# Experts' weights asked for by two engines: wide pairs by SyncE, narrow pairs by ScalarE, and the last unit's narrow pairs in places of wide ones

## The chip, the core and the metric

The kernel runs on one core of one Trainium2 chip. The metric is the device time of one launch in microseconds, the median over runs. Engines are named as in the profile: PE is TensorE (PEld its weight loads), DVE is VectorE, ACT is ScalarE, POOL is GpSimd, SP is SyncE.

## The reference

Three transformer-like blocks follow each other on 256 tokens of width 1024, in float32. The change lies in the second block's mixture of experts: a router picks 4 of 32 experts for each token, and each expert is two dense layers with a clipped SwiGLU between them.

```python
N_EXPERTS = 32
TOP_K = 4
D_FF_EXPERT = D_MODEL          # 1024
SWIGLU_ALPHA = 1.702
SWIGLU_LIMIT = 7.0
```

The first layer of an expert (`exp_w1`) is 1024 x 2048 (8 MB), the second (`exp_w2`) is 1024 x 1024 (4 MB). Each is multiplied once with the rows that the router sent to that expert, which are few, so that the 12 MB of weights of an expert are the larger cost to bring in.

## The kernel before

**Units.** The experts are worked through in units of up to 64 tokens. There are 32 units here, one for each expert (an expert with more than 64 tokens would add a unit). Unit `u` has a wide half (`widen`, the first layer, matmuls on line 2958) and a narrow half (`narrow`). The narrow half adds the previous unit's result into the output (`scatter`, line 2933), gathers the tokens of a later unit (line 2904), turns the hidden values (line 2986), and then multiplies with the second layer (line 3004). Between the wide half and the matmuls of line 3004, DVE and ACT clip, gate and copy; the last step of this is ACT's copy on line 3176.

**Weights in pairs.** The weights of a unit are twelve panels, moved as six pairs of 2 MB each, 128 partitions x 16 KB. Pairs 0 to 3 are wide, pairs 4 and 5 narrow (`TWICE` = 4, `PAIRS` = 6). The ring has ten places: pairs 0 to 3 have a place for even units and another for odd units, and pairs 4 and 5 have one place each for all units. Pairs 0 to 2 of even units lie in `ring`, which other stages use as six slots of 1 MB; all others lie in `expert_ring`. A transfer may start when PE has used up what was in the place before: PE raises `used` after each panel, 12 to a unit. PE waits for a pair on the semaphore of its place.

**Who asks.** Every weight transfer is asked for by SP, in the order in which its program has them, each behind its own wait for `used`. Up to unit 18 a turn of SP's loop has the wide pairs of one parity first, then the narrow pairs; from `AHEAD` = 9 pairs of units on (`in_turn`) a turn has the narrow pairs of the next unit first:

```python
def in_turn(v, before, even, odd):
    load(sp, v * 2 - 2, once, 1, before)
    load(sp, v * 2 - 2, twice, 0, even)
    load(sp, v * 2 - 1, once, 0, even)
    load(sp, v * 2 - 1, twice, 1, odd)
```

`load(sp, turn, pairs, odd, e)` waits until unit `turn` has used each of the `pairs` and then asks for the same pair of expert `e` into its place. `once` are pairs 4 and 5, `twice` are pairs 0 to 3. So the narrow pairs of unit u + 1 are asked for when unit u has used its own, and the wide pairs of unit u + 2 when unit u has used its own and SP has come past the narrow ones ahead of them. The transfers asked for by SP are one queue (q1 of the profile), those asked for by ACT are another (q10).

**The end.** The last unit (31) has odd places. Its narrow pairs are the last two weight transfers. Behind them SP asks for the first six panels (1 MB each, `w_in`) of the third block, into all six slots of `ring`. The third block starts when the last `scatter` is added.

Of the kernel before, what the change touches and what calls it, by code (L numbers as in the profile page):

```python
# [22 lines left out]
RING = 6  # L23
# [2817 lines left out]
def mixture_of_experts(core, h, halves_of_y, modulation, bias, ring, rw):  # L2841
# [3 lines left out]
    E, S = N_EXPERTS, UNIT  # L2845
# [5 lines left out]
    with ExitStack() as s:  # L2851
# [18 lines left out]
         glu_ready, sig_ready, hid_ready, hid_turned, hid_copied, bias_used, copied, scattered, added, turn) = (  # L2870
            core.counter("expert_" + n) for n in names)

        def pair_count(eng):
            return eng.value_load(unit_int[0:1, MAX_UNITS:MAX_UNITS + 1], min_val=E // 2, max_val=MAX_UNITS // 2)

        def last_pair(eng):
            return eng.value_load(unit_int[0:1, MAX_UNITS + 1:MAX_UNITS + 2], min_val=E // 2 - 1, max_val=MAX_UNITS // 2 - 1)

# [80 lines left out]
                                       start=False, stop=(j == 7))  # L2959
                mm.then_inc(used.sem, 1)  # L2960

        def panel(pe, u, v, odd, j):
            if j % 2 == 0:
                sig = ring.loaded_at(j // 2, odd)
                pe.wait_ge(sig.sem, (v if j // 2 < TWICE else u) * 16 + 16)
            return ring.panel(j, odd)

        def narrow(pe, u, v, odd, first=False, final=False):

            if not first:  # L2970
                scatter(pe, u)

            if not final:
                pe.wait_ge(picked.sem, picked.at(u + 2))
                gather(pe)
            pe.wait_ge(gates_picked.sem, gates_picked.at(u + 1))
            for b in range(NB):
                mm = pe.transpose(ps[:, 7, b * P:b * P + P], selg[:, b, :], ident)
            mm.then_inc(gates_turned.sem, 1)
            if first:  # L2980
                turn_columns(pe)
            pe.wait_ge(hid_ready.sem, hid_ready.at(u + 1))
            if not final:
                pe.wait_ge(xt_ready.sem, xt_ready.at(u + 2))
            for c in range(4):
                mm = pe.transpose(ps[:, 6, c * P:c * P + P], lin[:, c * P:c * P + P], ident)
            mm.then_inc(hid_turned.sem, 1)

            if not first:
                pe.wait_ge(added.sem, added.at(u * 4 + 1))  # L2990
            for out, at in halves:
                mm = pe.matmul(ps[out, 2, :], pick[:, :], bias[:, 2 * D + at:2 * D + at + 512], start=True, stop=False)
            mm.then_inc(bias_used.sem, 1)
            pe.wait_ge(gates_copied.sem, gates_copied.at(u + 1))
            if not final:
                turn_gathered(pe, u + 2)
            pe.wait_ge(hid_copied.sem, hid_copied.at(u + 1))
            for q in range(4):
                w = panel(pe, u, v, odd, 8 + q)
                for i in range(2):  # L3000
                    k = 2 * q + i
                    at_k = k % 4 * P + k // 4 * S
                    for out, at in halves:
                        mm = pe.matmul(ps[out, 2, :], hidt[:, at_k:at_k + S], w[:, i * D + at:i * D + at + 512],  # L3004
                                       start=False, stop=(k == DT - 1))
                mm.then_inc(used.sem, 1)

        def load(sp, turn, pairs, odd, e):
            for q in pairs:

                sp.wait_ge(used.sem, turn * PANELS + (2 * q + 2))
                sp.dma_start(ring.pair(q, odd), ring.weights(e, q)).then_inc(ring.loaded_at(q, odd).sem, 16)
        twice, once = range(TWICE), range(TWICE, PAIRS)

        def sb2(name, shape, dt=F32):
# [43 lines left out]
        with core.block() as block:  # L3059
# [85 lines left out]
            @block.scalar  # L3145
            def _(act):
                act.dma_start(rw[:, :, :], core.a["router"]).then_inc(core.const_loaded.sem, 16)
                core.load_table(act, ACT.Sqrt)
                act.wait_ge(gains_ready.sem, gains_ready.at(1))
                for k in range(DT):  # L3150
                    act.wait_ge(kept.sem, kept.at(k + 1))
                    act.activation(gained_tile[k], x[:, k, :], ACT.Copy, scale=core.gain[:, k:k + 1]).then_inc(gained.sem, 1)
                    if k < DT - 1:
                        act.activation(squares[:, k, :], x[:, k, :], ACT.Square).then_inc(squared.sem, 1)
                act.wait_ge(var_ready.sem, var_ready.at(1))
                act.activation(rs[:, :], rs[:, :], ACT.Sqrt).then_inc(rooted.sem, 1)
                act.wait_ge(rooted.sem, rooted.at(2))
                for half in range(2):
                    act.wait_ge(turned.sem, turned.at(half + 1))
                    for b in range(NB):  # L3160
                        act.activation(ht[:, b, 512 * half:512 * half + 512], ps[:, 2 * half + b, :], ACT.Copy,
                                       scale=rs[:, b:b + 1]).then_inc(copied_ht.sem, 1)
                copy_gathered(act, 1)
                act.wait_ge(shifted.sem, shifted.at(1))
                for b in range(NB):
                    ins = act.activation(g[:, b, :], lg[:, b, 0:E], ACT.Exp, bias=sm[:, b, 0:1])
                ins.then_inc(exped.sem, 1)
                core.load_table(act, ACT.Sigmoid)
                act.wait_ge(counted.sem, counted.at(1))
                def unit(u, final=False):  # L3170
                    act.wait_ge(glu_ready.sem, glu_ready.at(u + 1))
                    act.activation(sg[:, :], glu[:, :], ACT.Sigmoid, scale=SWIGLU_ALPHA).then_inc(sig_ready.sem, 1)  # L3172
                    if not final:
                        copy_gathered(act, u + 2)
                    act.wait_ge(hid_turned.sem, hid_turned.at(u + 1))
                    act.activation(hidt[:, :], ps[:, 6, :], ACT.Copy).then_inc(hid_copied.sem, 1)
                last = last_pair(act)
                with act.Fori(0, last) as v:
                    for odd in range(2):
                        unit(v * 2 + odd)  # L3180
                unit(last * 2)
                unit(last * 2 + 1, final=True)
                core.load_table(act, ACT.Sqrt)

# [141 lines left out]

            @block.sync
            def _(sp):
                def expert(u):
                    return sp.value_load(unit_int[0:1, bass.ds(u, 1)], min_val=0, max_val=E - 1)  # L3330
                issue_panels(core, sp, len(core.stream))
                ring.load_rest(sp)
                core.used += 4
# [1 line left out]
                    sp.wait_ge(used.sem, n + 1)  # L3335
                    sp.dma_start(ring.pair(0)[:, n * SLOT:n * SLOT + SLOT], ring.weights(2, 0)[:, n * SLOT:n * SLOT + SLOT]).then_inc(sig.sem, 16)
                load(sp, 0, twice[1:], 0, 2)
                load(sp, 0, range(4, PAIRS), 1, 1)
                load(sp, 1, twice, 1, 3)
                load(sp, 1, once, 0, 2)  # L3340
                with sp.Fori(2, AHEAD) as v:
                    load(sp, v * 2 - 2, twice, 0, v * 2)
                    load(sp, v * 2 - 2, once, 1, v * 2 - 1)
                    load(sp, v * 2 - 1, twice, 1, v * 2 + 1)
                    load(sp, v * 2 - 1, once, 0, v * 2)

                def in_turn(v, before, even, odd):
                    load(sp, v * 2 - 2, once, 1, before)
                    load(sp, v * 2 - 2, twice, 0, even)
                    load(sp, v * 2 - 1, once, 0, even)  # L3350
                    load(sp, v * 2 - 1, twice, 1, odd)
                load(sp, AHEAD * 2 - 2, twice[:1], 0, AHEAD * 2)
                load(sp, AHEAD * 2 - 2, once, 1, AHEAD * 2 - 1)
                load(sp, AHEAD * 2 - 2, twice[1:], 0, AHEAD * 2)
                load(sp, AHEAD * 2 - 1, once, 0, AHEAD * 2)
                load(sp, AHEAD * 2 - 1, twice, 1, AHEAD * 2 + 1)
                with sp.Fori(AHEAD + 1, E // 2 - 1) as v:
                    in_turn(v, v * 2 - 1, v * 2, v * 2 + 1)
                sp.wait_ge(counted.sem, counted.at(2))
                n = pair_count(sp)  # L3360
                with sp.Fori(E // 2 - 1, n) as v:
                    in_turn(v, expert(v * 2 - 1), expert(v * 2), expert(v * 2 + 1))
                last = last_pair(sp)
                load(sp, last * 2, once, 1, expert(last * 2 + 1))

                sp.wait_ge(used.sem, last * (2 * PANELS) + RING)
                switch_stream(core, STREAM_2)
                issue_panels(core, sp, RING)
        core.const_loaded.close(16)


PANELS, PAIRS, TWICE, AHEAD = 12, 6, 4, 9


class ExpertRing:
# [22 lines left out]
    def panel(self, j, odd=0):  # L3398
        return self.pair(j // 2, odd)[:, j % 2 * SLOT:j % 2 * SLOT + SLOT]
# [640 lines left out]
```

## Time and profile before

| what | value |
|---|---|
| median of 3 runs | 2319.06 us (2317.56 to 2319.47) |
| the profiled execution's own time | 2318.64 us |
| its span | 2316.8 us |
| granted TensorE clock, mean over the span | 0.995 |
| PE busy, whole span | 2217.1 us (96%) |
| DVE, ACT, POOL busy | 923.0, 382.1, 435.6 us |
| weight transfers of the experts | 144 + 47 pairs of 2 MB, and two of 1 MB |

The profiled execution's own time is 1.8 us above its span and 0.4 us below the median. The experts' units run from 1139.7 to 2050.6 us of the span. PE's busy share is an average over stages: what a change in the experts is worth is read in that stretch alone, from what PE waits for there and from how full the DMA engines are. Matmuls are counted as instructions; one float32 matmul of the program leaves two of them.

### The profile page before, as it was taken

To read this page: it belongs to the slowest core of one execution; us is meant where nothing else is said; L and a number is where in the kernel's file an instruction comes from. 1 tells how busy PE (TensorE), PEld (TensorE's weight loads), DVE (VectorE), ACT (ScalarE), POOL (GpSimd) and SP (SyncE) were. 2 spreads that over 40 slices of the span, in tenths; PEclk is the share of its full clock that TensorE was granted. 3 is DMA by queue.
4 is the path that set the end of the run, shared out by engine and by line. 5 is a ranking of instruction groups with operands and counts; after the bars stand their busy time and mean duration, and the time that the engine had idled before them with its cause. 6 is when DMAs were issued, how large, how long until landed. Compare 5 with 4: busy or idle time off the path is not lost. (4 is left out here: it accounts for less than half of the span.)

```text
span 2316.8 us, 35106 instructions
## 1 busy us (share of the span) xinstructions
PE 2217.1 (96%) x14557; PEld 1516.7 (65%) x14557; DVE 923.0 (40%) x1961; ACT 382.1 (16%) x856; POOL 435.6 (19%) x365
## 2 busy tenths in 40 slices
PE   8999999999999998999999999999999999999997
PEld 7888899987799987887633333333333333368786
DVE  4242465645444564626333333322333333252322
ACT  2210130124211023225200000000000000023321
POOL 0120498820088850012000000000000000000000
PEclk9999999999999999999999999999999999999999
DMA  7334754464864554323699999999999999953322
GB/s 264 128 125 145 239 168 164 161 234 170 326 217 164 164 182 163 120 111 152 247 426 427 428 428 428 428 428 427 405 426 430 426 429 428 427 238 130 127 82 82
DMA packets 61155, 619.36 MB, mean 267 GB/s; under 512 B 6800, under 2 KB 8080, under 8 KB 12304
## 3 DMA queue, kind: packets, MB, share of 16 engines
q1 hardware_dynamic: 59328, 611.08, 66.3%
q10 hardware_dynamic: 1712, 6.63, 0.8%
q8 instruction: 87, 1.43, 0.2%
q14 instruction: 28, 0.23, 0.0%
HBM read 616.63 MB, written 1.05 MB: 267 GB/s over the span
## 5 line engine op out<-in xcount | busy, mean ns | idle before, releaser
L2958 PE MATMUL ps<-expert_ring,moe_xg 128*64 128x512 f32 x1280 | 281.8, 593 | 9.8 <-DMA expert_ring<-we_dram 9.6
L3004 PE MATMUL ps<-expert_ring,mix_y 128*64 128x512 f32 x1024 | 228.5, 596 | 11.2 <-DMA expert_ring<-we_dram 11.2
L2958 PEld LDWEIGHTS ps<-expert_ring,moe_xg 128*64 128x64 f32 x1280 | 90.5, 137 | 189.8 <-issue 167.5
L466 PE MATMUL ps<-x_res,ring 128*128 128x256 f32 x896 | 201.3, 383 | 8.6 <-DMA x_res<-x_dram 8.6
L466 PEld LDWEIGHTS ps<-x_res,ring 128*128 128x128 f32 x896 | 169.8, 192 | 33.0 <-DMA ring<-w_in_dram 8.5
L3270 DVE TENSOR_SCALAR mix_y<-ps 128x512 f32<-128x512 f32 x32 | 22.1, 692 | 421.5 <-PE ps L2958 421.5
L2775 POOL COPY unscaled_x<-modulations 128x8 f32<-128x8 f32 x1 | 0.2, 198 | 936.0 <-POOLq L3059 936.0
L2958 PE MATMUL ps<-ring,moe_xg 128*64 128x512 f32 x768 | 168.2, 593 | 0.5 <-DVE moe_xg L2919 0.3
L3004 PEld LDWEIGHTS ps<-expert_ring,mix_y 128*64 128x64 f32 x1024 | 69.9, 137 | 147.4 <-issue 127.0
L466 PE MATMUL ps<-third_h,ring 128*128 128x256 f32 x704 | 160.1, 383 | 1.3 <-DVE third_h L3855 1.0
L625 POOL TENSOR_TENSOR seven_weights<-ring 128x512 f32<-128x512 f32 (+1 forms) x72 | 94.1, 1307 | 325.8 <-DVE seven_x_turned L641 289.1
L466 PEld LDWEIGHTS ps<-third_h,ring 128*128 128x128 f32 x704 | 133.8, 192 | 21.6 <-issue 2.2
L3172 ACT ACTIVATE mix_y<-mix_y 128x512 f32<-128x512 f32 x32 | 20.1, 630 | 739.8 <-DVE mix_y L3270 739.8
L2958 PEld LDWEIGHTS ps<-ring,moe_xg 128*64 128x64 f32 x768 | 54.6, 137 | 105.2 <-issue 98.9
L626 POOL TENSOR_TENSOR ring<-ring 128x512 f32<-128x512 f32 (+1 forms) x72 | 105.1, 1460 | 0.0
L430 PE MATMUL ps<-x_res,ring 128*128 128x128 f32 x768 | 102.1, 276 | 0.2
L430 PE MATMUL ps<-seven_x_turned,seven_weights 128*128 128x128 f32 x768 | 102.0, 276 | 0.2
L430 PE MATMUL ps<-seven_x_turned,ring 128*128 128x128 f32 x768 | 101.7, 275 | 0.2
L2943 DVE SCALAR_TENSOR_TENSOR x_res<-ps,modulations,x_res 128x256 f32<-128x256 f32 x248 | 99.7, 476 | 0.0
L466 PE MATMUL ps<-expert_ring,ring 128*128 128x256 f32 x416 | 95.3, 386 | 4.3 <-ACT expert_ring L279 4.3
L628 POOL TENSOR_TENSOR seven_weights<-seven_weights,ring 128x512 f32<-128x512 f32 (+1 forms) x72 | 98.2, 1363 | 0.0
L430 PEld LDWEIGHTS ps<-x_res,ring 128*128 128x128 f32 x768 | 93.7, 192 | 1.9 <-issue 0.8
(625 smaller groups left out, 3315.2 us busy)
## 6 DMA issues: line engine op xcount, KB each, us to landing
expert_ring<-we_dram SPq DMA_DIRECT2D x144, 2048.0 KB, 22.5
ring<-we_dram SPq DMA_DIRECT2D x47, 2048.0 KB, 25.6
ring<-w_in_dram SPq DMA_DIRECT2D x55, 1024.0 KB, 4.8
ring<-ffn_up_dram SPq DMA_DIRECT2D x44, 1024.0 KB, 5.1
ring<-ada_dram SPq DMA_DIRECT2D x36, 1024.0 KB, 4.8
ring<-w_out_dram SPq DMA_DIRECT2D x16, 1024.0 KB, 5.0
ring<-ffn_dn_dram SPq DMA_DIRECT2D x16, 1024.0 KB, 5.0
ring<-ple_g_dram SPq DMA_DIRECT2D x8, 1024.0 KB, 6.5
```

The costliest lines, as they stand in the source:

```text
L430: mm = pe.matmul(core.ps[:, bank, at:at + P], seven.weight(w, f, half, product, p), seven.moving(panel, sources[panel], k0, half, product, ...
L466: mm = pe.matmul(core.ps[:, bank_of[n, c], 0:TOK], w[:, k * PANEL + c * P:k * PANEL + c * P + P], sources[panel](k0 + k), start=(k0 + k == ...
L625: pool.tensor_tensor(s1, a21, a22, ALU.add).then_inc(summed.sem, 1)
L626: pool.tensor_tensor(a21, a11, a21, ALU.subtract).then_inc(summed.sem, 1)
L628: pool.tensor_tensor(s2, s1, a11, ALU.subtract).then_inc(summed.sem, 1)
L2775: pool.tensor_copy(self.xg[:, :, TOK], self.core.mod3[:, 0:8]).then_inc(*self.inc("columns"))
L2943: ins = dve.scalar_tensor_tensor(out=x[:, k, :], in0=ps[:, 2 + 2 * i + q, t * TOK:t * TOK + TOK], scalar=gate[:, k:k + 1], in1=x[:, k, :], ...
L2958: mm = pe.matmul(ps[out, bank, :], xg[:, j % 4, j // 4, :], w[:, bank * D + at:bank * D + at + 512], start=False, stop=(j == 7))
L3004: mm = pe.matmul(ps[out, 2, :], hidt[:, at_k:at_k + S], w[:, i * D + at:i * D + at + 512], start=False, stop=(k == DT - 1))
L3172: act.activation(sg[:, :], glu[:, :], ACT.Sigmoid, scale=SWIGLU_ALPHA).then_inc(sig_ready.sem, 1)
L3270: dve.tensor_scalar(glu[:, :], ps[:, 0, :], SWIGLU_LIMIT, None, ALU.min).then_inc(glu_ready.sem, 1)
```

## The change

SP keeps the wide pairs alone, in the order of the units. ACT asks for the narrow pairs of unit u + 1 after its own work for unit u, behind the same wait for `used` as before; for this it reads the number of the expert itself. The narrow pairs of the last unit no longer go to the places of narrow pairs: `load_moved` puts them into the even places of wide pairs 2 and 3, which no later unit needs, and waits only until unit 30 has used these. Of the third block's panels four are asked for instead of six ahead of its start, since slots 4 and 5 of `ring` are the even place of pair 2. They wait for unit 30's use of pair 2, as before.

```diff
-        def panel(pe, u, v, odd, j):
+        def panel(pe, u, v, odd, j, moved=False):
+            if moved:
+                q = j // 2 - 2
+                if j % 2 == 0:
+                    pe.wait_ge(ring.loaded_at(q, 0).sem, v * 16 + 32)
+                return ring.panel(2 * q + j % 2)
...
-                w = panel(pe, u, v, odd, 8 + q)
+                w = panel(pe, u, v, odd, 8 + q, final)
...
+        def load_moved(act, turn, e):
+            for q in range(TWICE, PAIRS):
+                place = q - 2
+                act.wait_ge(used.sem, turn * PANELS + (2 * place + 2))
+                act.dma_start(ring.pair(place), ring.weights(e, q)).then_inc(ring.loaded_at(place, 0).sem, 16)
...
-                with act.Fori(0, last) as v:
+                for u in range(2):
+                    unit(u)
+                    load(act, u, once, 0, u + 1)
+                act.wait_ge(counted.sem, counted.at(2))
+                last = last_pair(act)
+                with act.Fori(1, last) as v:
                     for odd in range(2):
                         unit(v * 2 + odd)
+                        load(act, v * 2 + odd, once, 0, expert(act, v * 2 + (odd + 1)))
                 unit(last * 2)
+                load_moved(act, last * 2, expert(act, last * 2 + 1))
                 unit(last * 2 + 1, final=True)
...
-                load(sp, 0, range(4, PAIRS), 1, 1)
                 load(sp, 1, twice, 1, 3)
-                load(sp, 1, once, 0, 2)
...
+                with sp.Fori(1, E // 2 - 2) as v:
+                    load(sp, v * 2, twice, 0, v * 2 + 2)
+                    load(sp, v * 2 + 1, twice, 1, v * 2 + 3)
                 sp.wait_ge(counted.sem, counted.at(2))
-                n = pair_count(sp)
-                with sp.Fori(E // 2 - 1, n) as v:
-                    in_turn(v, expert(v * 2 - 1), expert(v * 2), expert(v * 2 + 1))
                 last = last_pair(sp)
-                load(sp, last * 2, once, 1, expert(last * 2 + 1))
-
+                with sp.Fori(E // 2 - 2, last) as v:
+                    load(sp, v * 2, twice, 0, expert(sp, v * 2 + 2))
+                    load(sp, v * 2 + 1, twice, 1, expert(sp, v * 2 + 3))
                 sp.wait_ge(used.sem, last * (2 * PANELS) + RING)
                 switch_stream(core, STREAM_2)
-                issue_panels(core, sp, RING)
+                issue_panels(core, sp, 4)
```

The first place is the end of the experts on SP. Before, behind the loop: `we_dram` are the experts' weights (here the last unit's narrow pairs), `w_in_dram` the third block's first panels, and `moe_unit_int` holds the number of each unit's expert.

```order
L2877 TENSOR_LOAD moe_unit_int
L2877 ISA x2
L3330 ISA
L3330 TENSOR_LOAD moe_unit_int
L3330 ISA x2
L3011 ISA
L3012 ISA [waits expert_panel_used]
L3012 DMA expert_ring<-we_dram 128x4096
L3011 REGISTER_ALU
L3366 ISA
L251 DMA ring<-w_in_dram 128x2048 [waits expert_panel_used]
L251 DMA ring<-w_in_dram 128x2048 x5
```

Now, from the last wide pair of the last unit on:

```order
L3017 DMA expert_ring<-we_dram 128x4096
L3358 REGISTER_ALU
L3358 COMPARE_AND_BRANCH
L3361 ISA
L251 DMA ring<-w_in_dram 128x2048 [waits expert_panel_used]
L251 DMA ring<-w_in_dram 128x2048 x3
```

The narrow pairs are gone from SP, so the panels of the third block stand right behind the last unit's wide pairs in SP's queue.

The second place is ACT in the last unit but one. Before, its rows are the sigmoid, the copy of gathered tokens, and the copy of the turned hidden values (into `mix_y`):

```order
L3172 ACTIVATE mix_y<-mix_y 128x512 [waits expert_glu_ready]
L2914 REGISTER_ALU
L2915 ACTIVATE moe_xt<-ps 128x512 [waits expert_gathered]
L3176 ACTIVATE mix_y<-ps 128x512 [waits expert_hidden_turned]
```

Now ACT goes on, behind that copy, to the expert's number and the two narrow pairs of the last unit:

```order
L2912 ACTIVATE moe_xt<-ps 128x512 [waits expert_gathered]
L3186 ACTIVATE mix_y<-ps 128x512 [waits expert_hidden_turned]
L2960 ISA
L2960 TENSOR_LOAD moe_unit_int
L2960 ISA x2
L3022 ISA
L3023 ISA [waits expert_panel_used]
L3023 DMA ring<-we_dram 128x4096
L3022 REGISTER_ALU
L3023 DMA expert_ring<-we_dram 128x4096
```

What moved is the request for these two pairs: from SP, behind unit 30's use of its narrow pairs, to ACT, between its copy for unit 30 and its sigmoid for unit 31.

## Rows read from the trace of the kernel before

**Rows 1.** The page: PE, DMA share (tenths) and GB/s in 40 slices.

```profile
PE   8999999999999998999999999999999999999997
...
DMA  7334754464864554323699999999999999953322
GB/s 264 128 125 145 239 168 164 161 234 170 326 217 164 164 182 163 120 111 152 247 426 427 428 428 428 428 428 427 405 426 430 426 429 428 427 238 130 127 82 82
```

**Rows 2.** Windows: span, busy time by engine, PEclk, DMA share, GB/s.

```profile
1300.00:1400.00 100.00, 97.99 (x492) 36.13 (x490) 27.88 (x71) 5.47 (x9) 0.00 (x0) 1.00 1.01 428
...
1900.00:2000.00 100.00, 93.68 (x464) 33.54 (x462) 27.56 (x70) 5.47 (x9) 0.00 (x0) 1.00 1.01 428
...
1645.00:1650.00 5.00, 5.00 (x28) 1.70 (x26) 0.65 (x2) 0.00 (x0) 0.00 (x0) 1.00 0.55 180
...
3.00:8.00 5.00, 0.00 (x0) 0.00 (x0) 0.00 (x0) 0.00 (x0) 0.00 (x0) 1.00 1.00 419
...
14.00:19.00 5.00, 5.00 (x23) 2.48 (x22) 1.87 (x4) 1.67 (x2) 0.00 (x0) 1.00 1.01 426
...
460.00:464.00 4.00, 3.96 (x20) 3.96 (x21) 1.69 (x4) 0.28 (x1) 0.00 (x0) 0.57 0.00 0
```

**Rows 3.** PE's timeline, one unit: start, length, what, [idle before].

```profile
1622.40 13.90 PE L2958 MATMUL ps<-expert_ring,moe_xg 128*64 128x512 f32 x64
...
1642.69 7.09 PE L3004 MATMUL ps<-expert_ring,mix_y 128*64 128x512 f32 x32
...
1650.05 10.47 PE L2958 MATMUL ps<-ring,moe_xg 128*64 128x512 f32 x48
```

**Rows 4.** PE's timeline, units 30 and 31 and the third block's start.

```profile
2002.47 3.65 PE L2958 MATMUL ps<-expert_ring,moe_xg 128*64 128x512 f32 x16 [1.25 <-DMA expert_ring<-we_dram]
...
2012.51 7.09 PE L3004 MATMUL ps<-expert_ring,mix_y 128*64 128x512 f32 x32
...
2032.53 3.65 PE L2958 MATMUL ps<-expert_ring,moe_xg 128*64 128x512 f32 x16 [1.26 <-DMA expert_ring<-we_dram]
...
2040.63 7.08 PE L3004 MATMUL ps<-expert_ring,mix_y 128*64 128x512 f32 x32
...
2052.36 5.45 PE L457 MATMUL ps<-unscaled_x,ring 128*128 128x257 f32 x24 [1.79 <-ACT unscaled_x L2807]
...
2087.05 3.19 PE L466 MATMUL ps<-third_h,ring 128*128 128x256 f32 x14
```

**Rows 5.** SP's request for unit 31's last wide pair, and its landing.

```profile
L3012 SPq DMA_DIRECT2D expert_ring<-we_dram x1: 332/332/332, 1992.7 to 1992.7; - x1
...
DMA to landing us min/median/max: 39.8/39.8/39.8
```

**Rows 6.** The same for unit 31's last narrow pair.

```profile
L3012 SPq DMA_DIRECT2D expert_ring<-we_dram x1: 333/333/333, 2019.8 to 2019.8; - x1
...
DMA to landing us min/median/max: 22.5/22.5/22.5
```

**Rows 7.** The same for the pair that SP asked for at 1646.4.

```profile
L3012 SPq DMA_DIRECT2D expert_ring<-we_dram x1: 328/328/328, 1646.4 to 1646.4; - x1
...
DMA to landing us min/median/max: 7.7/7.7/7.7
```

**Rows 8.** ACT: its copy for unit 30, in the timeline.

```profile
2011.37 0.60 ACT L3176 ACTIVATE mix_y<-ps 128x512 f32<-128x512 f32 x1 [0.81 <-PE ps L2986]
```

**Rows 9.** ACT: its read of a number from SBUF (duration ns, start us).

```profile
L2877 ACTq TENSOR_LOAD <-moe_unit_int x1: 464/464/464, 1145.4 to 1145.4; - x1
```

**Rows 10.** DMA queues, 14 to 20 us: packets, MB, share of 16 engines.

```profile
q10 hardware_dynamic: 125, 1.53, 60.0%
q1 hardware_dynamic: 135, 1.01, 40.2%
```

**Rows 11.** PE's timeline where the granted clock fell.

```profile
460.04 1.81 PE L430 MATMUL ps<-first_arena,ring 128*128 128x128 f32 x8 [2.35 <-DVE seven_stage L658]
...
464.45 0.83 PE L430 MATMUL ps<-first_arena,ring 128*128 128x128 f32 x6
```

More of the change, by code:

```diff
@@ L2871, in mixture_of_experts @@
             core.counter("expert_" + n) for n in names)
-        def pair_count(eng):
-            return eng.value_load(unit_int[0:1, MAX_UNITS:MAX_UNITS + 1], min_val=E // 2, max_val=MAX_UNITS // 2)
         def last_pair(eng):
@@ L2960, in widen, with expert @@
                 mm.then_inc(used.sem, 1)
-        def panel(pe, u, v, odd, j):
+        def expert(eng, u):
+            return eng.value_load(unit_int[0:1, bass.ds(u, 1)], min_val=0, max_val=E - 1)
+        def panel(pe, u, v, odd, j, moved=False):
[4 more added lines that the diff above has]
+                return ring.panel(2 * q + j % 2)
             if j % 2 == 0:
@@ L3168, in _ @@
                 core.load_table(act, ACT.Sigmoid)
-                act.wait_ge(counted.sem, counted.at(1))
                 def unit(u, final=False):
@@ L3328, in _ @@
             def _(sp):
-                def expert(u):
-                    return sp.value_load(unit_int[0:1, bass.ds(u, 1)], min_val=0, max_val=E - 1)
                 issue_panels(core, sp, len(core.stream))
@@ L3337, in _ @@
                 load(sp, 0, twice[1:], 0, 2)
-                load(sp, 0, range(4, PAIRS), 1, 1)
                 load(sp, 1, twice, 1, 3)
-                load(sp, 1, once, 0, 2)
[L3341 to L3358, printed above, removed]
+                with sp.Fori(1, E // 2 - 2) as v:
+                    load(sp, v * 2, twice, 0, v * 2 + 2)
+                    load(sp, v * 2 + 1, twice, 1, v * 2 + 3)
                 sp.wait_ge(counted.sem, counted.at(2))
-                n = pair_count(sp)
-                with sp.Fori(E // 2 - 1, n) as v:
-                    in_turn(v, expert(v * 2 - 1), expert(v * 2), expert(v * 2 + 1))
                 last = last_pair(sp)
-                load(sp, last * 2, once, 1, expert(last * 2 + 1))
+                with sp.Fori(E // 2 - 2, last) as v:
+                    load(sp, v * 2, twice, 0, expert(sp, v * 2 + 2))
+                    load(sp, v * 2 + 1, twice, 1, expert(sp, v * 2 + 3))
                 sp.wait_ge(used.sem, last * (2 * PANELS) + RING)
                 switch_stream(core, STREAM_2)
-                issue_panels(core, sp, RING)
+                issue_panels(core, sp, 4)
         core.const_loaded.close(16)
-PANELS, PAIRS, TWICE, AHEAD = 12, 6, 4, 9
+PANELS, PAIRS, TWICE = 12, 6, 4
 class ExpertRing:
```

## The prediction

> **What bounds the kernel now.** I read the page's slices first. From the twentieth slice on, the DMA engines are full and move 426 to 428 GB/s while PE stands at nine tenths [rows 1], so two things are near their limit at once. The windows make it sharper: from 1300 to 1400 us PE is busy 97.99 us of 100, from 1900 to 2000 us only 93.68 us, and the DMA share is 1.01 in both [rows 2]. So the experts begin bound by PE, which eats up a stock of pairs that lie ready, and end bound by the DMA.
>
> The prices behind this: a pair is 2.097 MB, which at 428 GB/s takes 4.90 us, and a unit of six pairs 29.4 us. PE's timeline of a unit that waits for nothing has one wide start at 1622.40 and the next at 1650.05, so PE needs 27.65 us for a unit [rows 3]. PE gains 1.75 us a unit on the DMA until the stock is gone. Near the end, wide pair 3 of a unit is waited for: those of units 30 and 31 start at 2002.47 and 2032.53, each behind an idle 1.25 us that a DMA ended [rows 4].
>
> Then I read the landings. Wide pair 3 of unit 31 (call it W) was asked for at 1992.7 and landed 39.8 us later, at 2032.5, just where PE starts on it [rows 4, 5]. The last narrow pair landed at 2019.8 + 22.5 = 2042.3 [rows 6]. PE reaches the narrow matmuls at 2040.63, and that pair's half of them 3.5 us later [rows 4], so the narrow pairs are not waited for: the 8.1 us between W's start and 2040.63 hide them. In one queue, pairs land in the order in which they are used, W stands 9.8 us ahead of the end of the weight stream, and everything behind W follows it one for one.
>
> **The change part by part.** The bytes are the same, and the DMA is already full, so asking earlier gives nothing in the middle. What can move is the end of the stream and W's place in it.
>
> *The end of the stream.* SP's waiting order leaves one gap: between 1645 and 1650 only 180 GB/s are moved, and the pair asked for at 1646.4 lands 7.7 us later, 2.8 us more than its transfer takes [rows 2, 7]. The missing bytes are worth (1 - 180/428) x 5 = 2.9 us. With wide pairs asked for as soon as their places are free, this gap goes. How much of it reaches the last landing lies between 0 and 2.9 us; I take the middle, 1.4 us. The stream then ends at 2040.9.
>
> *Two queues.* No expert pair of before goes through ACT's queue, so the sharing is read from the start of the kernel: in 14 to 20 us, with both queues filled, q10 moved 125 packets and q1 135 [rows 10]. They take turns, packet by packet, and with equal packets of 16 KB each queue gets half. A narrow pair then takes 9.8 us instead of waiting behind the wide ones; meanwhile wide pairs come at half speed.
>
> *The steady state, counted from the moment L at which wide pair 3 of a unit lands.* The narrow matmuls start at L + 10.1 (2002.47 to 2012.51), their first half ends 3.5 us later, the second at L + 17.1 [rows 4]. The narrow pairs of the next unit are asked for at these two moments (0.2 us for the wait), begin to move 2.8 us later [rows 7], and take 19.6 us together at half rate: from L + 16.6 to L + 36.2. They are needed at L + 39.5 and later, so they come in time. The next wide pair 3 is due at L + 29.4. Up to then the narrow pairs have taken 12.8 us of half rate, 6.4 us of the whole stream, which before they took after it. So PE stands 6.4 us later in the stream than before, less the gap: +5.0 us. For unit 30, L is 2007.4.
>
> *The last unit.* ACT's copy ends 9.5 us after L (2011.37 + 0.60, against 2002.47) [rows 4, 8]. Reading the expert's number takes 0.46 us by the nearest row [rows 9], with its register work 0.9 us. The waits on `used` are long met. So the last narrow pairs are asked for at L + 10.4 and move from L + 13.2 = 2020.6. The stream has 20.3 us left, 4.1 pairs, two of which are the narrow ones and 2.1 are wide. At half rate the narrow ones are done after 19.6 us, at 2040.2, and W lands last, at 2040.9. Before it was 2032.5: **+8.4 us**. The two narrow pairs have only changed sides with W, but they were hidden behind 8.1 us of work, and W has 18 us of work behind it. The four panels of the third block stand behind W in SP's queue and delay nothing here.
>
> *The clock.* PE begins the wide half at L + 17.5 = 2024.9 and has three pairs done 10.4 us later, at 2035.3, then idles 5.6 us for W. Before the start at 460.04 it idled 2.35 us, and from 460 to 464 us the granted clock was 0.57 on the mean: 3.4 us at 1.2 instead of 2.4 GHz. Eight matmuls took 1.81 us there, against six in 0.83 us after [rows 2, 11]. An idle 1.79 us at 2052.36 is followed by 24 in 5.45 us [rows 4], the full-speed length. I put a fall behind W's wait, 3.4 / 2 = **+1.7 us**; its bounds are 0 and, with a second fall, 3.4. Falls in the middle of the stretch cost nothing as long as 27.65 + 1.7 stays under 29.4.
>
> *Costed at nothing.* ACT's requests: its next job is the sigmoid some 14 us of wide matmuls later; without this cover, about 1 us a unit. SP's wide requests: SP does nothing else. Panels 4 and 5 of the third block, asked for only after its start at 2062, are needed no sooner than 2087.05 + 10 [rows 4]; a panel in an empty queue takes under the 7.7 us of a pair [rows 7], so 25 us cover it. The first panel lands 2.5 us behind W, at 2043.4, and is needed at 2062.
>
> Sum: 8.4 + 1.7 = 10.1 us on the profiled execution's own 2318.64, **2328.7 us**. That execution lies 0.4 us below the median, so I say 2329.
>
> **The rivals.** 0.2% of this kernel is 4.6 us, about what a measurement can tell from no change.
>
> *The two queues together move more than one did.* This is the rival on the other side. Some 890 us of full stream lie ahead of W, so each 1% of rate moves it 8.9 us. At 433 GB/s the loss is gone; from 435 on the kernel is faster by over 0.2%: 2329 - 14.5 = 2314. For it: nothing shows that one queue's 428 is the engines' limit. Against it: with two queues filled, 426 GB/s at mixed packet sizes and 419 at the start [rows 2]. I give 0.12 for a result within 0.2% and 0.10 for faster.
>
> The Trainium skill ("DMA: Bandwidth & Descriptors", section "Issuing engines are not separate DMA queues") says that transfers started by different engines run on the same 16 DMA engines and interleave, and that only issue time is saved. By this rule the rate stays, as in the sum. The same page, section "Where 436 GB/s comes from", puts the ceiling at 435 GB/s; an estimate from that page's figure, with the whole ceiling reached, would be about 1.6% of 890 us, 14 us off the sum.
>
> *Two queues move less.* 419 against 428 is 2%, but the packets there were of 8 KB. If 0.5 to 1% is lost, 4 to 9 us come on top: 2333 to 2338. I give 0.13.
>
> *Requests are served by time, not in turn.* Then W keeps its place, but the last narrow pairs stand behind the four panels (9.8 us), and the last lands at 2050.7. Its matmuls end at 2054.2 instead of 2047.7: +6.5 us, 2325. Against it are the packet counts [rows 10]. I give 0.05.
>
> *ACT's queue gets clearly less than half.* The narrow pairs have 3 us in hand in each unit. At a third of the rate they would land at L + 45 and more, PE would wait for them while the ten places are full, and the DMA would run dry: at least 5 us a unit as long as it lasts, 2340 or more. I give 0.05.
>
> *The last narrow pairs come late enough for W to pass them.* Each us by which their request is later brings W one us forward; 6 us would be needed to come under 0.2%. No row speaks for it: 0.05, within 0.2%.
>
> **How the numbers follow.** The likeliest case has 0.50, and its own range is 2325 to 2332 (the gap 0 to 2.9, the clock 0 to 3.4). Slower: 0.50 + 0.13 + 0.05 + 0.05 = 0.73. Within 0.2%: 0.12 + 0.05 = 0.17. Faster: 0.10. The range 2319 to 2337 leaves out the faster case, the case of a starved queue and half of the ends of the rate cases, some 0.2.
>
> **What would show it.** In the changed profile: no gap near 1645 us; DMA share 1.0 and 426 to 429 GB/s from 1200 us until W lands; q10 with about a third of the experts' bytes; waits for a DMA in the wide matmuls alone, none in the narrow ones; W landing near 2041, behind an idle PE of 4 to 6 us, and a fall of the granted clock to 1.2 GHz right there; the third block's first matmul near 2062. I am wrong if the rate with two queues differs from 428 by over 0.5%, if the narrow half waits, or if W lands before the last narrow pair.

## The result, and the profile after

The changed kernel takes **2327.74 us** (median of 9 runs, 2322.27 to 2332.49), the kernel before, run beside it, 2319.06 us (2317.32 to 2321.2): ratio **1.0035, 95% interval 1.0027 to 1.0044**. It is slower by 0.35%. The profiled execution took 2328.73 us, with a span of 2326.9 us, 10.1 us more than before, and a mean clock of 0.991.

The page's slices, parts 3 and 6 of the changed kernel:

```profile
PE   8999999999999998999999999999999999989997
...
GB/s 264 127 124 145 240 174 161 155 235 190 316 200 167 160 182 172 116 104 186 248 426 428 428 428 428 428 428 428 428 428 428 428 428 428 427 144 132 127 79 85
...
q1 hardware_dynamic: 50400, 481.06, 52.8%
q10 hardware_dynamic: 10640, 136.65, 14.0%
...
expert_ring<-we_dram SPq DMA_DIRECT2D x82, 2048.0 KB, 45.7
expert_ring<-we_dram ACTq DMA_DIRECT2D x61, 2048.0 KB, 14.5
```

Where the slices of [rows 1] had 405 GB/s in the middle of the experts, all slices now have 426 to 428. The gap is gone and the rate has not moved. ACT's queue brings 61 of some 190 pairs, a third.

Windows of the changed kernel (span, then busy time by engine, PEclk, DMA share, GB/s): the middle, the place of the former gap, PE's idle time before W, and W's matmuls:

```profile
1300.00:1400.00 100.00, 97.98 (x492) 36.16 (x490) 27.90 (x71) 5.47 (x9) 0.00 (x0) 1.00 1.01 428
1640.00:1660.00 20.00, 17.87 (x78) 5.55 (x74) 1.19 (x4) 0.00 (x0) 0.00 (x0) 0.91 1.01 428
2036.00:2041.00 5.00, 0.19 (x2) 0.19 (x4) 0.00 (x0) 0.00 (x0) 0.00 (x0) 0.67 0.99 413
2041.00:2045.00 4.00, 4.00 (x12) 1.19 (x12) 0.00 (x0) 0.00 (x0) 0.00 (x0) 0.55 1.01 422
```

PE's timeline of the changed kernel, the last two units and the start of the third block:

```profile
2007.09 3.65 PE L2955 MATMUL ps<-expert_ring,moe_xg 128*64 128x512 f32 x16 [0.90 <-DMA expert_ring<-we_dram]
...
2017.13 7.09 PE L3009 MATMUL ps<-expert_ring,mix_y 128*64 128x512 f32 x32
...
2024.48 10.77 PE L2955 MATMUL ps<-expert_ring,moe_xg 128*64 128x512 f32 x48
2040.81 5.50 PE L2955 MATMUL ps<-expert_ring,moe_xg 128*64 128x512 f32 x16 [5.56 <-DMA expert_ring<-we_dram]
...
2050.78 3.65 PE L3009 MATMUL ps<-ring,mix_y 128*64 128x512 f32 x16
...
2062.52 5.45 PE L457 MATMUL ps<-unscaled_x,ring 128*128 128x257 f32 x24 [1.79 <-ACT unscaled_x L2807]
```

Beside [rows 4], W's start has moved from 2032.53 to 2040.81 and the idle time in front of it has grown from 1.26 to 5.56 us. The sixteen matmuls on W take 5.50 us where sixteen of the same shape take 3.65 at 2007.09: the window 2041 to 2045 has a granted clock of 0.55. The record of the fall to half speed, 1.2 instead of 2.4 GHz, runs from 2037.7 to 2044.6, so that 3.8 us of it lie on W's matmuls. The narrow matmuls wait for no DMA.

The requests for W (by SP) and for the last narrow pair (by ACT), with their way to landing; two answers on the changed kernel:

```profile
L3017 SPq DMA_DIRECT2D expert_ring<-we_dram x1: 333/333/333, 1982.2 to 1982.2; - x1
DMA to landing us min/median/max: 58.6/58.6/58.6
...
L3023 ACTq DMA_DIRECT2D expert_ring<-we_dram x1: 339/339/339, 2017.4 to 2017.4; - x1
DMA to landing us min/median/max: 22.7/22.7/22.7
```

W is asked for 10.5 us sooner than in [rows 5] and lands 8.3 us later, at 2040.8. The last narrow pair is asked for 35.2 us after W and lands 0.7 us ahead of it, at 2040.1. How it could overtake is in the queues between 2020 and 2030:

```profile
q1 hardware_dynamic: 149, 2.18, 51.0%
q10 hardware_dynamic: 140, 2.10, 49.8%
```

The columns are packets, MB and the share of the 16 engines. ACT's queue, with two pairs, moves 2.10 MB, and SP's queue, with all that stands in it, 2.18 MB: each has half.

**How the times are compared below.** The experts' first wide matmul starts within 2 us of the same time in all kernels (1139.71 before, 1139.73 after). I count from it to three places of PE's timeline: the start on wide pair 3 of unit 30 (L), the start on W, and the third block's first matmul (the end). Before, these are 862.8, 892.8 and 912.65 us. In the changed kernel L is +4.6, W +8.3, and the end +10.1, all of what the span shows. A unit without a wait takes 27.65 us [rows 3] and 19.8 us lie between W's start and the end [rows 4]; so 2.4 us of the 30.06 between L and W were waits before.

### The profile page after: what moved, and what is told of

The parts are those of the page before. It is cut to its first block and busy times, and to the rows that moved or that the text cites. A ratio compares the mean times of both kernels' runs of the same rounds, so it can differ in the third digit from the quotient of the medians.

```text
span 2326.9 us, 35246 instructions
## 1 busy us (share of the span) xinstructions
PE 2223.5 (96%) x14557; PEld 1519.2 (65%) x14557; DVE 923.3 (40%) x1961; ACT 382.3 (16%) x857; POOL 435.6 (19%) x365
## 5 line engine op out<-in xcount | busy, mean ns | idle before, releaser
L2955 PE MATMUL ps<-expert_ring,moe_xg 128*64 128x512 f32 x1280 | 290.5, 607 | 25.0 <-DMA expert_ring<-we_dram 24.9
L3009 PE MATMUL ps<-expert_ring,mix_y 128*64 128x512 f32 x1008 | 223.3, 595 | 0.0
```

Source lines behind the costliest of these rows:

```text
L2955: mm = pe.matmul(ps[out, bank, :], xg[:, j % 4, j // 4, :], w[:, bank * D + at:bank * D + at + 512], start=False, stop=(j == 7))
```

## The experiments

Each was run beside the kernel before on the same chip (medians of 2319.38 for the first four, 2318.86 for the next four, 2320.13 for the last).

**Only the last narrow pairs go back to SP, behind W.** Everything else is as changed, their places too.

```diff
                 unit(last * 2)
-                load_moved(act, last * 2, expert(act, last * 2 + 1))
...
                     load(sp, v * 2 + 1, twice, 1, expert(sp, v * 2 + 3))
+                load_moved(sp, last * 2, expert(sp, last * 2 + 1))
                 sp.wait_ge(used.sem, last * (2 * PANELS) + RING)
```

> The changed kernel, but the last unit's two narrow pairs are asked for by SyncE, behind the last unit's wide pairs, in one queue. Theory (only the place of the last wide pair in the stream costs): that pair lands 9.8 us ahead of the stream's end, near 2031, PE reaches it near 2035.3 and does not wait, so the wait of 5.6 us and the fall of the clock (1.85 us) both go: about 7.4 us less than the changed kernel's 2328.7, some 2321; 2.7 us above before stay, since PE still stands later in the stream. Rival (the two queues cost something all along, by rate or by waits in the narrow halves): 2326 to 2329, little moved. Rival (the narrow pairs now bind): they would be waited for near 2045 and give back more than 1 us.

Measured 2318.9 us (2317.68 to 2322.44, 11 runs), ratio 0.9999 [0.999, 1.0008]. PE's timeline:

```profile
2006.01 3.66 PE L2955 MATMUL ps<-expert_ring,moe_xg 128*64 128x512 f32 x16 [0.91 <-DMA expert_ring<-we_dram]
...
2023.40 13.90 PE L2955 MATMUL ps<-expert_ring,moe_xg 128*64 128x512 f32 x64
...
2053.48 5.45 PE L457 MATMUL ps<-unscaled_x,ring 128*128 128x257 f32 x24 [1.79 <-ACT unscaled_x L2807]
```

All 64 wide matmuls of the last unit run in one piece. Two queues up to unit 30 leave L at +4.1 us, as in the changed kernel. With W in time the 2.4 us of waits of the last unit fall away, and the end is at +1.7. So the two queues up to unit 30 leave 1.7 us above the kernel before, and the other 8.4 us of the loss hang on ACT's last two requests. (What the two queues cost against a tail in one queue is larger; the seventh experiment has it.) The timed result is 2 us under my number. The 2.7 us above before that I expected lie outside the interval, which ends at 1.9 us; the 1.7 us of the trace lie inside.

**The last narrow pairs asked for by ACT, in their own places.** Their request then waits until unit 30 has used its narrow pairs.

```diff
-                w = panel(pe, u, v, odd, 8 + q, final)
+                w = panel(pe, u, v, odd, 8 + q)
...
-                load_moved(act, last * 2, expert(act, last * 2 + 1))
+                load(act, last * 2, once, 1, expert(act, last * 2 + 1))
```

> The changed kernel, but the last unit's narrow pairs go to the narrow places as in every other unit, asked for by ScalarE when unit 30 has used its own. Theory: they start to move 3.4 us later and share the stream with fewer wide pairs; the last wide pair lands near 2038.2 instead of 2040.8, PE waits 2.9 us for it, the clock still falls: about 2.6 us less, 2326. Rival (it is the moving of these pairs that costs the 8.7 us): back to before, 2319. Rival (own places are too late for the narrow half): 2330 or more, with a wait in the last narrow half.

Measured 2324.68 us (2320.58 to 2330.12, 11 runs), ratio 1.0019 [1.001, 1.0028]. PE's timeline:

```profile
2009.79 5.35 PE L2955 MATMUL ps<-expert_ring,moe_xg 128*64 128x512 f32 x16 [3.33 <-DMA expert_ring<-we_dram]
...
2028.88 13.90 PE L2955 MATMUL ps<-expert_ring,moe_xg 128*64 128x512 f32 x64
...
2058.95 5.45 PE L457 MATMUL ps<-unscaled_x,ring 128*128 128x257 f32 x24 [1.79 <-ACT unscaled_x L2807]
```

The size came near my number, by another way than I wrote down. The two requests go out at 2025.4 and 2028.8 of this trace; counted from the first wide matmul that is 7.2 and 10.0 us later than in the changed kernel. W, counted as above, lands 6.6 us sooner and is not waited for at all. The +5.2 us of this trace lie one unit earlier: L is at +6.0, behind a wait of 3.33 us and a clock fall (5.35 us for sixteen matmuls), and then -2.4 + 1.7 follow. Waits of 3.3 to 3.4 us came in every second or third unit of this trace, and where in that sequence unit 30 stands is not something the experiment sets. What it shows is that W moves forward when the narrow request comes later; it doesn't give the price of the moved places to a microsecond.

**PE is kept busy while it waits for W.** 22 small matmuls (44 instructions), whose result nobody reads, stand ahead of panel 6 of the last unit.

```diff
             for j in range(8):
+                if j == 6:
+                    for _ in range(fill):
+                        pe.matmul(ps[:, 6, 0:P], ident, core.m("ones"), start=True, stop=True)
                 w = panel(pe, u, v, odd, j)
...
-                widen(pe, last * 2 + 1, last, 1)
+                widen(pe, last * 2 + 1, last, 1, fill=22)
```

> The changed kernel with 22 idle-time matmuls of 128 x 128 on constants, about 5 us in all, ahead of the last unit's wide pair 3, into a bank that nothing reads; they fill PE's wait. Theory (the clock falls because PE idles, and the last wide pair's matmuls pay for it): the matmuls take 3.65 us instead of 5.50 and the kernel comes to about 2326.9, 1.8 us less. Rival (the fall has another cause, or what follows is not bound by PE): 2328.7, unchanged. If the fill is longer than the wait of a run, it adds up to 1 us.

Measured 2326.24 us (2323.86 to 2327.28, 10 runs), ratio 1.0028 [1.0019, 1.0038]. PE's timeline:

```profile
2034.62 5.18 PE L2954 MATMUL ps<-mat 128*128 128x128 f32 x44
2040.23 3.65 PE L2958 MATMUL ps<-expert_ring,moe_xg 128*64 128x512 f32 x16 [0.44 <-DMA expert_ring<-we_dram]
...
2060.06 5.45 PE L457 MATMUL ps<-unscaled_x,ring 128*128 128x257 f32 x24 [1.79 <-ACT unscaled_x L2807]
```

W is at +8.0 us as in the changed kernel, but its matmuls take 3.65 us instead of 5.50, and from W's start to the end it is 19.8 us, the length of before, against 21.7. The clock's part is thus 1.9 us and W's lateness the rest. This rests on the traces: the interval of the ratio overlaps that of the changed kernel.

**The old single queue, with the wide pairs first up to the end.** From the kernel before: the order that it had up to unit 18 stays to the last unit.

```diff
-                with sp.Fori(2, AHEAD) as v:
+                with sp.Fori(2, E // 2 - 1) as v:
...
                 with sp.Fori(E // 2 - 1, n) as v:
-                    in_turn(v, expert(v * 2 - 1), expert(v * 2), expert(v * 2 + 1))
+                    load(sp, v * 2 - 2, twice, 0, expert(v * 2))
+                    load(sp, v * 2 - 2, once, 1, expert(v * 2 - 1))
+                    load(sp, v * 2 - 1, twice, 1, expert(v * 2 + 1))
+                    load(sp, v * 2 - 1, once, 0, expert(v * 2))
```

> The kernel before, one queue, but its first order of requests (wide pairs of unit u + 2, then narrow pairs of unit u + 1) is kept to the end, without the other order from unit 18 on. All bytes and the rate stay. Theory (the order of landing counts, and only at the end): the last unit's wide pairs land ahead of unit 30's narrow ones, PE waits in narrow halves, and behind the landing of unit 30's last narrow pair near 2031 (9.8 us ahead of an end at 2040.9) PE has 32.4 us of work to the end of the block against 18.1 us behind the last wide pair before: 12.9 us above before, about 2332. Rival (a full stream is all that counts): 2318 to 2319, a little under before by the gap near 1645 us.

Measured 2331.1 us (2328.14 to 2334.01, 5 runs), ratio 1.0048 [1.0035, 1.0062]. PE's timeline:

```profile
2025.14 3.65 PE L3004 MATMUL ps<-expert_ring,mix_y 128*64 128x512 f32 x16 [0.23 <-DMA expert_ring<-we_dram]
2030.19 3.65 PE L3004 MATMUL ps<-expert_ring,mix_y 128*64 128x512 f32 x16 [1.40 <-DMA expert_ring<-we_dram]
...
2034.11 13.90 PE L2958 MATMUL ps<-expert_ring,moe_xg 128*64 128x512 f32 x64
...
2064.19 5.45 PE L457 MATMUL ps<-unscaled_x,ring 128*128 128x257 f32 x24 [1.79 <-ACT unscaled_x L2807]
```

One queue, the same bytes at 428 GB/s up to 2025 us, and +12.0 us. Here the narrow pairs of unit 30 stand behind the wide pairs of unit 31, and PE waits for them. Behind them the stream has a gap (244 GB/s from 2025 to 2030), since the last two pairs are asked for only at 2029.0 and 2034.1, but PE waits for neither. The loss doesn't need two queues. It comes from the order in which the last pairs land; a second queue is one way to spoil that order.

**Only the last narrow pairs go to ACT, in the kernel before.** This is one part of the change alone, the counterpart of the first experiment.

```diff
                 unit(last * 2)
+                act.wait_ge(counted.sem, counted.at(2))
+                load(act, last * 2, once, 1, act.value_load(unit_int[0:1, bass.ds(last * 2 + 1, 1)], min_val=0, max_val=E - 1))
...
-                load(sp, last * 2, once, 1, expert(last * 2 + 1))
```

> The kernel before with one change: the last unit's two narrow pairs, same places and same moment of request, are asked for by ScalarE instead of SyncE. Theory (two filled queues take turns, so these two pairs pass the last wide ones): they move from 2019.2 on, when 2.7 wide pairs are left, and take 19.6 us at half rate; the last wide pair lands 9.8 us later, near 2042.3, PE waits 11 us for it and the clock falls behind: 9.8 + 1.85 = 11.7 us above before, 2331. Rival (requests are served by time, whatever the queue): 2319.1, unchanged. Rival (the loss needs the whole scheme, all narrow pairs on the second queue): under 3 us.

Measured 2327.53 us (2325.82 to 2332.74, 5 runs), ratio 1.0049 [1.0035, 1.0062]. The requests for W and for the last narrow pair, and PE's timeline:

```profile
L3012 SPq DMA_DIRECT2D expert_ring<-we_dram x1: 332/332/332, 1991.3 to 1991.3; - x1
DMA to landing us min/median/max: 49.8/49.8/49.8
...
L3012 ACTq DMA_DIRECT2D expert_ring<-we_dram x1: 349/349/349, 2018.3 to 2018.3; - x1
DMA to landing us min/median/max: 21.5/21.5/21.5
```

```profile
2023.58 3.65 PE L2958 MATMUL ps<-expert_ring,moe_xg 128*64 128x512 f32 x16 [1.55 <-DMA expert_ring<-we_dram]
2033.39 5.15 PE L2958 MATMUL ps<-expert_ring,moe_xg 128*64 128x512 f32 x16 [6.16 <-DMA expert_ring<-we_dram]
2041.17 3.65 PE L2958 MATMUL ps<-expert_ring,moe_xg 128*64 128x512 f32 x16 [2.63 <-DMA expert_ring<-we_dram]
```

W's way to landing grows from 39.8 us [rows 5] to 49.8: 10.0 us, the time of two pairs (9.8). Besides this only the third block's panels are asked for sooner, and they land behind W; so this is what a short, late request in a second queue does to the backlog of the first. The wait is spread over wide pairs 2 and 3. The clock falls around the longer one, and what that costs is taken from the second wait, since W lands when it lands. So the trace has +10.3 us and not the 11.7 that I summed. The medians stand 8.7 us apart, the ratio of 1.0049 would be 11.4 us: five runs place it no closer.

**W in two halves.** In the kernel before, W is asked for as two transfers of 1 MB, and PE starts on the first half when that has landed (the edit of PE's side is left out here).

```diff
+        def load_halves(sp, turn, odd, e):
+            sp.wait_ge(used.sem, turn * PANELS + 8)
+            for n, sig in enumerate((half_loaded, ring.loaded_at(3, odd))):
+                sp.dma_start(ring.pair(3, odd)[:, n * SLOT:n * SLOT + SLOT], ring.weights(e, 3)[:, n * SLOT:n * SLOT + SLOT]).then_inc(sig.sem, 16)
...
-                    in_turn(v, expert(v * 2 - 1), expert(v * 2), expert(v * 2 + 1))
+                    load(sp, v * 2 - 2, once, 1, expert(v * 2 - 1))
+                    load(sp, v * 2 - 2, twice, 0, expert(v * 2))
+                    load(sp, v * 2 - 1, once, 0, expert(v * 2))
+                    load(sp, v * 2 - 1, twice[:3], 1, expert(v * 2 + 1))
+                    load_halves(sp, v * 2 - 1, 1, expert(v * 2 + 1))
```

> The kernel before with the last unit's last wide pair as two transfers of 1 MB with a semaphore each, so that PE may begin its first panel when half has landed (written for 32 units). Theory (the landing of the last wide pair sets the end): the wait of 1.25 us goes and the second panel ends 1.75 us behind the landing instead of 3.5: 1.75 us less, 2317.3. Rival (something behind it, the narrow pairs, binds next): less than half of that.

Measured 2317.02 us (2314.87 to 2321.76, 11 runs), ratio 0.9996 [0.9987, 1.0005]: no difference that the runs can tell. The trace ends at -1.4 us, where I had -1.75. PE waits 1.07 us for wide pair 2 of the last unit and not for W, and the last narrow pair lands only 0.3 us ahead of its matmuls.

**Two queues first, one queue in order at the end.** From the changed kernel: ACT asks for narrow pairs up to unit 26 only; from there on SP asks for everything, in the order of use, the last narrow pairs behind W. The edit, with `TAIL` = 13:

```diff
-                with act.Fori(1, last) as v:
+                with act.Fori(1, TAIL) as v:
...
-                load_moved(act, last * 2, expert(act, last * 2 + 1))
...
-                with sp.Fori(E // 2 - 2, last) as v:
+                with sp.Fori(TAIL, last) as v:
+                    load(sp, v * 2, once, 0, expert(sp, v * 2 + 1))
                     load(sp, v * 2, twice, 0, expert(sp, v * 2 + 2))
+                    load(sp, v * 2 + 1, once, 0, expert(sp, v * 2 + 2))
                     load(sp, v * 2 + 1, twice, 1, expert(sp, v * 2 + 3))
+                load_moved(sp, last * 2, expert(sp, last * 2 + 1))
```

> The changed kernel up to unit 26; from there SyncE asks for everything in the order of use, narrow pairs of unit u + 1 ahead of wide pairs of unit u + 2, and the last narrow pairs, still in places of wide ones, come last. Theory (the middle costs nothing as long as the stream is full; only what lands ahead of the last wide pair counts, and PE catches up 1.75 us a unit once the order is that of use): the 6.4 us are caught up in four units, the gap near 1645 us stays away, so 1.4 us less than before, 2317.7, and about 10 us less than the changed kernel. Rival (the two queues in the middle leave something behind): 2320 or more.

Measured 2316.47 us (2314.86 to 2317.74, 11 runs), ratio 0.9991 [0.9982, 1.0]. PE's timeline:

```profile
2002.46 3.65 PE L2955 MATMUL ps<-expert_ring,moe_xg 128*64 128x512 f32 x16 [0.70 <-DMA expert_ring<-we_dram]
...
2031.88 3.65 PE L2955 MATMUL ps<-expert_ring,moe_xg 128*64 128x512 f32 x16 [1.25 <-DMA expert_ring<-we_dram]
```

W's start is at -2.6 us and the end too. The last weights land 2.6 us sooner than before, close to the 2.9 us that the gap near 1645 was worth [rows 2]; that gap is what the first part of the change removes, so with the last pairs in order nearly all of it reaches the end.

Beside the first experiment, which keeps ACT's narrow pairs up to unit 30, L is 6.1 us sooner (-2.0 against +4.1) and the end 4.3 us sooner (-2.6 against +1.7). So the second queue is free up to unit 26, from where PE catches up, but not in the last units; the 6.1 us are near the 6.4 that I had for PE's place in the stream. The timed ratios of the two kernels, 0.9991 and 0.9999, have intervals that overlap, so this split rests on the traces too.

**Both together.** The edits of the last two.

> The two last kernels together. Theory: both gains add, 3.1 us less than before, near 2316.0; PE then has nothing in hand at the last narrow pair, which may show a short wait. Rival (they overlap): 2317 to 2318.

Measured 2315.97 us (2313.68 to 2317.03, 11 runs), ratio 0.9989 [0.998, 0.9998]. PE's timeline:

```profile
2018.74 14.22 PE L2962 MATMUL ps<-expert_ring,moe_xg 128*64 128x512 f32 x64
```

The last unit's wide half runs in one piece, and the end is at -2.9 us. The 3.1 us that I summed come near, but the two gains do not add: the traces of the parts have -2.6 and -1.4, together -4.0. The last weights land 1.3 us sooner than before here, where the tail alone had 2.6, and the last narrow pair 0.3 us ahead of its matmuls. The median is the lowest of the kernels here, some 3 us under the one before; the interval only just leaves 1 out, and it overlaps those of the last two.

**The changed kernel again.**

> The changed kernel itself, a second profile. Open: its runs spread over 10 us, those of before over 4. Theory (the waits on wide pairs 3 settle in another pattern from launch to launch, with other falls of the clock among them, and the last wide pair still lands last): the stream's weights end at the same time after unit 0's start (902.6 us in the first profile), the last wide pair is waited for 4 to 7 us, and the median is again near 2328. Rival (the last wide pair does not always land last): its wait differs by more than 3 us between the two profiles.

Measured 2328.59 us (2326.65 to 2330.16, 5 runs), ratio 1.0038 [1.0025, 1.0052]; the end is at +9.7 us. PE's timeline:

```profile
2005.02 3.65 PE L2955 MATMUL ps<-expert_ring,moe_xg 128*64 128x512 f32 x16 [0.98 <-DMA expert_ring<-we_dram]
...
2038.71 6.07 PE L2955 MATMUL ps<-expert_ring,moe_xg 128*64 128x512 f32 x16 [5.54 <-DMA expert_ring<-we_dram]
```

The requests for W and for the last narrow pair, and their way to landing:

```profile
L3017 SPq DMA_DIRECT2D expert_ring<-we_dram x1: 333/333/333, 1980.0 to 1980.0; - x1
DMA to landing us min/median/max: 58.7/58.7/58.7
...
L3023 ACTq DMA_DIRECT2D expert_ring<-we_dram x1: 339/339/339, 2015.4 to 2015.4; - x1
DMA to landing us min/median/max: 23.8/23.8/23.8
```

The wait for W comes back in the same place and size. Two things differ. W lands at 2038.7 and the last narrow pair at 2039.2: this time W passes it, by 0.5 us, against what I expected. W's start is at +7.3 us, 1 us sooner than in the first trace, and from there to the end it is 22.2 us instead of 21.7: sixteen matmuls take 6.07 us, 2.4 more than at full clock. The weights end 900.6 us after the first wide matmul; the first trace has 901.0 (the 902.6 in my expectation is the kernel before's).

## Why the prediction was right, point by point

*The end of the stream.* I took 1.4 us off for the gap. The last weights land 901.0 us after the first wide matmul in the changed kernel, 900.6 in its second trace, 900.0 with the tail in order and 901.2 with both edits, against 902.6 before: 1.3 to 2.6 us. The step holds; my middle of 1.4 was on the small side.

*Two queues take turns.* 149 packets against 140 and 2.18 MB against 2.10 in 10 us, and 428 GB/s in both kernels from 1200 to 1640 and from 1660 to 2030 us. This leaves nothing of the rivals in which the queues together move more or less, or ACT's queue gets clearly less than half. By the Trainium skill ("DMA: Bandwidth & Descriptors", section "Issuing engines are not separate DMA queues") the engines' transfers interleave on the same 16 DMA engines; the slices and the packet counts agree.

*The steady state.* L was to be 2007.4 and was 2007.04 (its landing). PE's lateness there was +4.6 by the trace, where I had +5.0. That it is the second queue's sharing is shown from two sides: the first experiment has it too (+4.1) without ACT's last requests, and with one queue from unit 26 on L is at -2.0.

*The last unit.* The last narrow pair was to be asked for at L + 10.4; it was, at 2017.45. It was to be done at 2040.2, and landed at 2040.1; W was to land at 2040.9, and landed at 2040.8. PE stood idle 5.56 us, where I had 5.6. The cause is shown from both sides: with these two requests taken back alone, the end returns to +1.7 us; with these two requests moved alone, it goes to +10.3. The rival by time of request is excluded, since the pair asked for 35 us after W overtook it. W passing the last narrow pair was a rival, and a sign by which I would call myself wrong. In the first trace it did not happen, by 0.6 us; in the second it did, by 0.5 us. My margin was 0.7 us, so the order of these two landings was a toss-up that I gave as fixed. It hardly touches the price, since both queues share the stream up to there and W is late either way (+8.3 and +7.3 us). The rival's mechanism is real: with requests 7.2 to 10.0 us later, W was 6.6 us sooner, but then the loss came in unit 30.

*The clock.* +1.7 was right to 0.2: the third experiment puts it at 1.9 us. The way there was partly luck. I took a fall of 3.4 us from [rows 11] to lie wholly on W's matmuls; the fall here lasted 6.8 us, began in PE's idle time, and 3.8 us of it lay on them. In the second trace 4.9 us did, for 2.4 us. The other falls of the changed kernel, four of them between 1566 and 1891, cost nothing at the end, as W's arrival is set by the stream.

*Costed at nothing.* The third block's first panel landed 2.5 us behind W and its first matmul waited for ACT alone. Panels 4 and 5, asked for at 2061.3 and 2061.7, landed at 2066.4 and 2070.4, well ahead of their use.

*The sum.* 8.4 + 1.7 = 10.1 against 8.26 + 1.88 = 10.14 in the first trace and 7.3 + 2.4 = 9.7 in the second, and 8.7 us between the medians. The mechanism and its size were right; an agreement to 0.1 us is luck, as the two terms move by 1.0 and 0.5 us from one execution to the next. The stream's gain of 1.6 to 2.0 us in the changed kernel came from the gap that went, not from a higher rate, and the order of the last six pairs took back more than that.

## What to carry to other kernels

With the DMA full, the second queue added no bandwidth here (428 GB/s with one and with two). It only changed the order in which transfers land: a late request in the empty queue took half of the stream from the backlog of the other. Up to unit 26 that was free, since PE caught up afterwards; kept up to unit 30 it cost 4.3 us, and done for the last two pairs another 8.4. What is used last should land last, so the last transfers belong in one queue in the order of their use, from a few units before the end. Work out for each of them how much work hides it and how much lies behind it: here 8 us of cover for the narrow pairs were traded for a wide pair with 18 us of work behind it.

## What the runs showed that I had not expected

With two queues the waits for wide pair 3 alternate from unit to unit, where the kernel before has 1.15 to 1.51 us in each of its late units. PE's timeline of the changed kernel, all waits for a DMA from 1720 to 1900:

```profile
1743.11 5.35 PE L2955 MATMUL ps<-expert_ring,moe_xg 128*64 128x512 f32 x16 [2.17 <-DMA expert_ring<-we_dram]
...
1801.30 3.65 PE L2955 MATMUL ps<-expert_ring,moe_xg 128*64 128x512 f32 x16 [0.98 <-DMA expert_ring<-we_dram]
...
1831.30 3.65 PE L2955 MATMUL ps<-expert_ring,moe_xg 128*64 128x512 f32 x16 [2.13 <-DMA expert_ring<-we_dram]
...
1860.11 3.65 PE L2955 MATMUL ps<-expert_ring,moe_xg 128*64 128x512 f32 x16 [0.95 <-DMA expert_ring<-we_dram]
...
1890.09 5.35 PE L2955 MATMUL ps<-expert_ring,moe_xg 128*64 128x512 f32 x16 [2.12 <-DMA expert_ring<-we_dram]
```

And a wait of about 2.1 us sometimes brings the clock down and sometimes not: after 2.17 and 2.12 us (1743, 1890) the sixteen matmuls take 5.35 us, after 2.13 us (1831) and after another 2.17 us at 1978 they take 3.65. In the unit behind such a fall PE waits for no DMA: what the slow clock costs is taken from the next wait. Two windows of the changed kernel, around the wait of 3.14 us at 1567 and that of 2.13 us at 1831:

```profile
1565.00:1570.00 5.00, 2.68 (x8) 0.84 (x10) 0.00 (x0) 0.00 (x0) 0.00 (x0) 0.67 1.01 429
...
1828.00:1834.00 6.00, 3.87 (x20) 1.14 (x18) 0.00 (x0) 0.00 (x0) 0.00 (x0) 1.00 1.01 429
```

The waits of 0.70 to 0.98 us in this trace were not followed by a fall, and none between 1 and 2.1 us occurred in it. Longer waits do not decide it either: in the second experiment seven waits have 3.28 to 3.39 us, and four of them were followed by a fall. Before W the record of the fall begins 2.5 us into PE's idle time and lasts 6.83 us. What decides between two waits of equal length stays open; no run was made for it.

The first nine runs of the changed kernel scatter more than those of the kernel before beside them, 2322 to 2332 us against 2317 to 2321. The repeat does not bear this out: five runs within 3.5 us against nine within 5.7. Whether the waits vary more from run to run is not known, since only single executions are profiled.
